# A two-block language-model forward pass on one core: three projection blocks of the next stage are run chunk by chunk while the norm before them arrives, at four boundaries

## Chip, core and metric

The kernel runs on one core of one Trainium2 chip. The metric is device time in microseconds (us) of one launch. TensorE (PE) multiplies matrices, ScalarE (ACT), VectorE (DVE) and GpSimd (POOL) work element by element, and SyncE (SP) issues the loads of the weights.

## What is computed

The reference runs 272 tokens (16 meta tokens and 256 others) of width 1024 through two blocks, all in float32. The first block has a state-space mixer, a latent-attention mixer and two squared-ReLU MLPs. The second block, on 256 tokens, is where the change lies. Cut to what matters:

```python
def second_block(x, mem, ...):
    mem_n = rms_norm_2(mem, mem_norm_gain)              # 256 memory tokens
    for layer in range(2):
        g = norm_gains[layer]
        hn = rms_norm_2(x, g[0])
        y = mlstm_mixer(hn, ...) if layer == 0 else stick_breaking_mixer(hn, ...)
        x = x + rms_norm_2(y, g[1])
        y = memory_cross_attention(rms_norm_2(x, g[2]), mem_n, w_q, w_kv, w_o)
        x = x + rms_norm_2(y, g[3])
        y = swiglu_ffn(rms_norm_2(x, g[4]), w_gate_up, w_down)
        x = x + rms_norm_2(y, g[5])
```

## The kernel before

Activations lie with features on the 128 partitions and tokens along the row, so 1024 features are 8 **chunks** of 128x256. A projection is cut into **blocks** of 128 output features. A block (`pe_block`) is 8 chunks times 3 matmuls of 256 columns: float32 operands are split into a high and a low part, and high x high, high x low and low x high are summed in one PSUM bank. The weights of a block pass through three steps: SP loads 512 KB into one of 4 `RAW` buffers, ACT writes the high part `WH` (`act_split`, signal `hi`), DVE writes the low part `WL` (`dve_split`, signal `lo`). ACT may write slot i mod 4 only when the block four earlier has been used (`use`), and splits up to 3 blocks ahead of the block it is handling; DVE splits 2 ahead. The order of all blocks is one list, `PLAN`.

All synchronisation is by semaphores in an order written by hand for each engine; an engine that waits holds back all that is queued behind it.

A **boundary** is what stands between two stages: a projection `post` (xo0, fd0, sbo, xo1) gives Y in 8 blocks; its squares are summed over features by PE with a matrix of ones (a **product**; `pe_feed` for the early ones, `pe_rest` for the last); ACT takes Ln and Exp of the sum (`act_table`); DVE refines the reciprocal root in three operations (`dve_newton`, signal `rms`). Then for each chunk m, DVE scales Y, DVE (even m) or POOL (odd m) adds it to X, ACT writes the high part of the next norm's input `HNH` and its square, and DVE writes the low part `HNL` (signal `hn`). The next stage's blocks multiply these unscaled chunks, and its own sum of squares (8 more products into bank 7) gives a factor by which DVE multiplies each block when it evicts it. So the next stage's first eviction waits for products, Ln, Exp and the three refining operations again.

While PE would wait at a boundary it is given **fills**: key (k) and value (v) blocks of the memory cross-attention, `xkv0` and `xkv1`, 16 blocks each, which depend on no norm of x. A v block is followed by two transposes (`pe_v_end`). Before the change `xkv1` is dealt out as: k0 and k1 in the last steps of cross-attention 0, k2 to k7 at boundary xo0, v0 to v3 at the end of the stick-breaking mixer, v4 to v7 at boundary sbo. Boundaries fd0 and xo1 have none. The first block of the next stage starts when the five early products of that norm are in.

The stages in order are xq0 and attention core 0, xo0, ffn0 (`gu0` blocks, then `fd0`), `sbqkv` and the stick-breaking core, sbo, xq1 and attention core 1, xo1, ffn1. The first places of the four stages behind the boundaries are blocks gu0 0, sbqkv 0, xq1 0, gu1 0.

## Time and profile before

| | |
|---|---|
| median of 3 runs | 1770.18 us (1765.0 to 1772.51) |
| the profiled execution | 1770.89 us, span 1769.1 us |
| PE busy | 1690.5 us of the span |
| DVE, ACT, POOL busy | 1186.5, 936.5, 332.4 us |
| TensorE clock granted, mean | 0.98 of full |

Time outside the span is 1.8 us. The granted clock is given as a share of 2.4 GHz, so 0.50 in a row is the level of 1.2 GHz. A matmul record lasts longer than the distance to the next one, because matmuls are pipelined; the distance between starts is what a matmul costs. A product of float32 squares is two records.

### The profile page before, as it was taken

The page shows a single profiled execution, that of the slowest core. Times are in us where ns is not written, and L with a number is a line of the kernel's source. Part 1 is how long each engine was busy: PE and PEld are TensorE (multiplying, and loading weights), DVE is VectorE, ACT ScalarE, POOL GpSimd, SP SyncE. Part 2 cuts the span into 40 slices and gives each one's busy share as a digit, 9 for nine tenths or more (in the row PEclk, how much of TensorE's full clock was granted, in tenths as well). Part 3 has the DMA queues.
Part 4 walks back from the last instruction along what each step waited for, and adds up shares of the span by engine and source line. Part 5 has one row for each costly group of instructions (what it writes and reads, how often), then busy time and mean ns, then how long its engine had stood idle before and what let it go on. Part 6 is the DMA issues. An engine that isn't in the chain of part 4 may idle for free.

```text
span 1769.1 us, 32699 instructions
## 1 busy us (share of the span) xinstructions
PE 1690.5 (96%) x13204; PEld 1615.9 (91%) x13204; DVE 1186.5 (67%) x2027; ACT 936.5 (53%) x1659; POOL 332.4 (19%) x304
## 2 busy tenths in 40 slices
PE   6999999999999989999999999999989999989997
PEld 6898889999997889999888999999979998889997
DVE  6999887555577745556577665866666667476665
ACT  5677765544455646544555444544455644454443
POOL 0100011243412112345111100000252110000025
PEclk8999999999999999999999999999999999989999
DMA  5433334555532245555334534455644343335663
GB/s 179 132 120 108 120 108 143 166 171 177 179 93 80 81 140 184 187 187 185 129 118 146 167 120 155 155 170 184 181 147 136 127 156 118 107 118 172 185 184 106
DMA packets 76325, 257.47 MB, mean 146 GB/s; under 512 B 8464, under 2 KB 12560, under 8 KB 75920
## 3 DMA queue, kind: packets, MB, share of 16 engines
q1 hardware_dynamic: 76176, 255.39, 45.1%
q8 instruction: 105, 1.72, 0.4%
q14 instruction: 44, 0.36, 0.1%
HBM read 254.31 MB, written 1.05 MB: 144 GB/s over the span
## 4 chain that ended last, share of the span: by engine, by line
PE 77%; DVE 12%; ACT 6%; issue 4%; POOL 1%; DMA 0%; POOLq 0%; DVEq 0%; SPq 0%; ACTq 0%
PE pb L140 75%; DVE WL L159 2%; DVE TMP L171 2%; DVE SCR L171 2%; ACT SCR L149 1%; ACT L156 1%; DVE SCR L159 1%; PE pb L143 1%; ACT WH L149 1%; DVE HNL L171 1%; POOL SCR L159 1%; ACT TMP L149 1%; ACT ASH L149 1%; DVE ASL L171 0%; ACT Rbuf L149 0%
## 5 line engine op out<-in xcount | busy, mean ns | idle before, releaser
L140 PE MATMUL pb<-HNH,WH 128*128 128x256 f32 (+1 forms) x2120 | 613.9, 290 | 6.1 <-DVE WL L159 1.9
L159 DVE TENSOR_TENSOR WL<-RAW,WH 128x1024 fp32r<-128x1024 f32 (+4 forms) x514 | 604.9, 1177 | 10.4 <-ACT WH L149 10.0
L140 PE MATMUL pb<-HNH,WL 128*128 128x256 f32 (+1 forms) x2120 | 603.1, 284 | 0.0
L140 PE MATMUL pb<-HNL,WH 128*128 128x256 f32 (+1 forms) x2120 | 602.8, 284 | 0.0
L149 ACT ACTIVATE WH<-RAW 128x1024 fp32r<-128x1024 f32 (+4 forms) x514 | 507.2, 989 | 154.7 <-PE pb L140 147.1
L140 PE MATMUL pb<-ASH,WH 128*128 128x256 f32 (+1 forms) x1688 | 493.4, 292 | 11.1 <-DVE WL L159 7.1
L140 PE MATMUL pb<-ASH,WL 128*128 128x256 f32 (+1 forms) x1688 | 483.2, 286 | 0.0
L140 PE MATMUL pb<-ASL,WH 128*128 128x256 f32 (+1 forms) x1688 | 482.9, 286 | 0.0
L140 PEld LDWEIGHTS pb<-HNH,WH 128*128 128x128 f32 x2120 | 402.1, 190 | 14.3 <-issue 6.8
L140 PEld LDWEIGHTS pb<-HNH,WL 128*128 128x128 f32 x2120 | 402.4, 190 | 0.0
L140 PEld LDWEIGHTS pb<-HNL,WH 128*128 128x128 f32 x2120 | 400.6, 189 | 1.0
L140 PEld LDWEIGHTS pb<-ASH,WH 128*128 128x128 f32 x1688 | 324.3, 192 | 19.0 <-issue 7.9
L140 PEld LDWEIGHTS pb<-ASL,WH 128*128 128x128 f32 x1688 | 323.5, 192 | 1.0
L140 PEld LDWEIGHTS pb<-ASH,WL 128*128 128x128 f32 x1688 | 324.1, 192 | 0.0
L140 PE MATMUL pb<-SCR 128*64 128x128 f32 (+12 forms) x880 | 124.5, 321 | 10.7 <-DVE SCR L171 4.2
L140 PEld LDWEIGHTS pb<-SCR 128*64 128x64 f32 (+6 forms) x880 | 91.1, 162 | 34.1 <-issue 11.2
L159 DVE TENSOR_TENSOR ASL<-TMP,ASH 128x256 fp32r<-128x256 f32 (+1 forms) x108 | 46.5, 430 | 109.2 <-ACT ASH L149 109.2
L159 POOL TENSOR_TENSOR SCR<-SCR,TMP 128x256 f32<-128x256 f32 x48 | 59.9, 1248 | 312.9 <-DVE TMP L159 312.9
L159 POOL TENSOR_TENSOR SCR<-SCR 128x512 f32<-128x512 f32 (+2 forms) x36 | 43.5, 1217 | 377.8 <-ACT SCR L149 239.8
L159 POOL TENSOR_TENSOR X<-X,TMP 128x272 f32<-128x272 f32 (+1 forms) x64 | 96.4, 1506 | 87.9 <-DVE TMP L159 87.9
L159 DVE TENSOR_TENSOR TMP<-pb,Rbuf 128x256 f32<-128x256 f32 (+1 forms) x112 | 47.9, 428 | 94.8 <-PE pb L140 94.8
L140 PE MATMUL pb<-SQ,cp 128*128 128x256 f32 (+2 forms) x274 | 83.8, 421 | 25.9 <-ACT SQ L149 22.5
(149 smaller groups left out, 1454.3 us busy)
## 6 DMA issues: line engine op xcount, KB each, us to landing
RAW<-in_w_gu SPq DMA_DIRECT2D x88, 512.0 KB, 3.8
RAW<-in_w_up SPq DMA_DIRECT2D x64, 512.0 KB, 3.5
RAW<-in_w_down SPq DMA_DIRECT2D x64, 512.0 KB, 3.5
RAW<-in_w_ssd SPq DMA_DIRECT2D x48, 512.0 KB, 3.5
RAW<-in_w_xkv SPq DMA_DIRECT2D x32, 512.0 KB, 3.5
RAW<-in_w_mlin SPq DMA_DIRECT2D x24, 512.0 KB, 3.5
RAW<-in_w_fd SPq DMA_DIRECT2D x32, 384.0 KB, 3.0
RAW<-in_w_sbqkv SPq DMA_DIRECT2D x24, 512.0 KB, 4.1
```

The lines of the kernel that those rows point to most:

```text
L140: return self.eng.matmul(o, l, r, start=start, stop=stop, skip_group_check=skip) if self.eng else Nothing()
L143: return self.eng.transpose(o, i, ident) if self.eng else Nothing()
L149: return self.eng.activation(o, i, f, bias=bias, scale=scale)
L156: self.eng.preload_act_table_set(name)
L159: return self.eng.tensor_tensor(o, a, b, op) if self.eng else Nothing()
L171: return self.eng.scalar_tensor_tensor(out=o, in0=a, scalar=s, in1=b, op0=op0, op1=op1)
```

## The change

At the four boundaries xo0, fd0, sbo and xo1, `pe_post_norm` gives way to `pe_wave`. It runs at most one fill, the last products of the post norm, the other fills, and then a **wave**: as each normed chunk c arrives, three matmuls of block 0 and three of block 1 of the next stage on it; from c = 4 on also six matmuls of block 2, on chunks 2c-8 and 2c-7. The waves write PSUM banks 3, 4 and 5, and each waits for that bank's last reader (`wave_free`). The last three products follow the wave. ACT splits one weight block more before the norms (`act_split_to`), DVE one before its refining operations, one behind its first `HNL`, and at the start of the next stage the one for block 3.

The memory blocks `xkv1` are dealt out anew: k0, k1, k2 in the last steps of cross-attention 0; k3, k4 at xo0; k5, k6, k7 at fd0; v0 to v3 as before; v4, v5 at sbo; v6, v7 in the last steps of cross-attention 1. Since the FFN has overwritten the normed memory by then, k5 to k7 read a copy in `ASH`/`ASL` 0 to 7 that `act_mem2` and `dve_mem2` make during the last eight `fd0` blocks: 8 more ACT and 8 more DVE instructions of 128x256. In cross-attention 1 the core no longer waits for v7 at its start; head h waits for value block 2h+1 before its last product.

```diff
     p += xkv[0][0:7] + out("mlo", xkv[0][7:16])
-    p += [("xq0", 0, m) for m in range(8)] + xkv[1][0:2] + out("xo0", xkv[1][2:8])
-    p += ffn(0)
-    p += [("sbqkv", 0, m) for m in range(24)] + xkv[1][8:12] + out("sbo", xkv[1][12:16])
-    p += [("xq1", 0, m) for m in range(8)] + out("xo1", [])
+    p += [("xq0", 0, m) for m in range(8)] + xkv[1][0:3] + out("xo0", xkv[1][3:5])
+    p += ffn(0) + xkv[1][5:8]
+    p += [("sbqkv", 0, m) for m in range(24)] + xkv[1][8:12] + out("sbo", xkv[1][12:14])
+    p += [("xq1", 0, m) for m in range(8)] + xkv[1][14:16] + out("xo1", [])
     p += ffn(1)
...
+WAVES = [(name, m) for name in ("gu0", "sbqkv", "xq1", "gu1") for m in range(3)]
...
-            elif AT["ssd", 0, FIRST] <= i - 3 <= AT["ssd", 0, 47]:
-                q.wait_ge(*ssd_read(i - 4))
+            elif (name, m) in WAVES:
+                for w in wave_free(name, m):
+                    q.wait_ge(*w)
             elif i >= 3:
-                q.wait_ge(*(eva if PLAN[i - 3][0] in ("up0", "up1", "wk") else evd)[i - 3])
+                j = bank_before(i)
+                if AT["ssd", 0, FIRST] <= j <= AT["ssd", 0, 47]:
+                    q.wait_ge(*ssd_read(j - 1))
+                else:
+                    q.wait_ge(*(eva if PLAN[j][0] in ("up0", "up1", "wk") else evd)[j])
...
-                "xo0": [(1, "k", m) for m in range(2, 8)], "sbo": [(1, "v", c) for c in range(4, 8)],
-                "xo1": [], "fd0": [], "fd1": []}
+                "xo0": [(1, "k", 3), (1, "k", 4)], "fd0": [(1, "k", m) for m in range(5, 8)],
+                "sbo": [(1, "v", 4), (1, "v", 5)], "xo1": [], "fd1": []}
+        WAVE = {"xo0": "gu0", "fd0": "sbqkv", "sbo": "xq1", "xo1": "gu1"}
+        def wave_free(name, m):
+            return {"gu0": ([xex[0, 3, 1]], [dm[3]], [xp[0, 3]]),
+                    "sbqkv": ([evd[AT["gu0", 0, 0]]], [evd[AT["gu0", 0, 1]]], [evd[AT["gu0", 0, 2]]]),
+                    "xq1": ([zd[7, 0]], [zd[7, 1]], [xvc[1, 4]]),
+                    "gu1": ([xex[1, 3, 1]], [evd[AT["xq1", 0, 1]]], [xp[1, 3]])}[name][m]
...
+        def pe_wave(q, post):
+            fill, nxt, name = FILL[post], NEXT[post], WAVE[post]
+            for f in fill[:1]:
+                pe_fill(q, *f)
+            pe_rest(q, post, T2)
+            for f in fill[1:]:
+                pe_fill(q, *f)
+            xs = hn_chunks(nxt)
+            ids = [q.block(name, 0, m) for m in range(3)]
+            for c in range(8):
+                for m in range(2):
+                    if c == 0:
+                        pe_bank_free(q, ids[m])
+                        q.wait_ge(*lo[ids[m]])
+                    pe_chunks(q, ids[m], T2, xs, c, c + 1)
+                if c == 4:
+                    pe_bank_free(q, ids[2])
+                    q.wait_ge(*lo[ids[2]])
+                if c > 3:
+                    pe_chunks(q, ids[2], T2, xs, 2 * c - 8, 2 * c - 6)
+                pe_feed(q, nxt, c, T2, rms[post])
+            pe_rest(q, nxt, T2)
...
+        def act_wave(q, post):
+            fill, nxt, name = FILL[post], NEXT[post], WAVE[post]
+            n = POSTS.index(post)
+            for f in fill[:1]:
+                act_fill(q, *f)
+            act_table(q, post, row(RPO, T2), T2, 1024, ynorm[POSTS[n - 1], 7])
+            act_split_to(q, q.i + 3)
+            for m in range(1, 9):
+                act_norm(q, nxt, m - 1, x_added(post, m - 1), use[AT[HNFREE[nxt]]])
+                if m in (2, 4) and m // 2 < len(fill):
+                    act_fill(q, *fill[m // 2])
...
+        def dve_wave(q, post):
+            fill, nxt, gi, name = FILL[post], NEXT[post], GAIN[post], WAVE[post]
+            for f in fill[:1]:
+                dve_fill(q, *f)
+            dve_split_to(q, q.i + 2)
+            r = row(RPO, T2)
+            dve_newton(q, post, r, SUMS[:, 0:T2], 1024, rough[post])
+            q.wait_ge(*rms[post])
+            for m in range(10):
+                if m < 8:
+                    q.wait_ge(*y_ready(post, m))
+                    q.stt(Y[:, m, :], Y[:, m, :], cc("ng", gi * 8 + m, 1), r, ALU.mult, ALU.mult).then_inc(*ynorm(post, m))
+                if m % 2 and m < 8:
+                    d = X[:, m - 1, NMETA:T1]
+                    q.wait_ge(*ynorm[post, m - 1])
+                    q.wait_ge(*x_before(post, m - 1))
+                    q.tt(d, d, Y[:, m - 1, :], ALU.add).then_inc(*xpd(post, m - 1))
+                if m > 1:
+                    dve_norm(q, nxt, m - 2)
+                if m == 2:
+                    dve_split_to(q, q.i + 3)
+                if m in (3, 5) and m // 2 < len(fill):
+                    dve_fill(q, *fill[m // 2])
+                    dve_split_to(q, q.i + 2)
...
+        def act_mem2(q, c):
+            act_part(q, "mem2", c, ASH[:, c, 0:T2], MR[:, c, :], use[AT["fd0_5", 0, 7]], scale=cc("memn", c, 1))
...
         def xa_fill(l, n):
-            return [(1, "k", n - 9)] if l == 0 and n > 8 else []
+            if l == 0:
+                return [(1, "k", n - 8)] if n >= 8 else []
+            return [(1, "v", n - 2)] if n in (8, 9) else []
...
-                    q.wait_ge(*xvc[l, 7])
...
+                q.wait_ge(*xvc[l, 2 * h + 1])
...
-            pe_v_end(q, l, 7)
+            if l == 0:
+                pe_v_end(q, 0, 7)
             for m in range(8):
-                pe_block(q, f"xq{l}", 0, m, T2, xs)
-                if m == 0:
+                if l == 0 or m > 2:
+                    pe_block(q, f"xq{l}", 0, m, T2, xs)
+                if l == 0 and m == 0:
                     pe_rest(q, key, T2)
                 for h, k in xa_cores(m):
                     pe_xa_core(q, l, h, k)
             for n in range(8, 11):
                 for f in xa_fill(l, n):
                     pe_fill(q, *f)
+                if l and n == 10:
+                    pe_v_end(q, 1, 7)
                 for h, k in xa_cores(n):
                     pe_xa_core(q, l, h, k)
-            pe_post(q, f"xo{l}", as_chunks(key, 0, 8, T2, 2), rms[key])
-            pe_post_norm(q, f"xo{l}")
+            pe_post(q, f"xo{l}", as_chunks(key, 0, 8, T2, 2), xvc[1, 7] if l else rms[key])
+            pe_wave(q, f"xo{l}")
...
                         if x == 0:
+                            dve_split_to(q, i + 3)
                             dve_newton(q, key, R, SUMS[:, 0:T2], 1024, rough[key])
                             q.wait_ge(*rms[key])
...
+                            if 2 * (c0 + j) + e > 2:
+                                pe_block(q, f"gu{l}", 0, 2 * (c0 + j) + e, T2, xs)
```

The DVE queue at the start of ffn0 before the change: the refining operations of the norm, the eviction of gate block 0 (`TMP<-pb,Rbuf`), and what follows, with what each row waits for.

```order
L171 SCALAR_TENSOR_TENSOR Rbuf<-TMP,Rbuf 128x256 [waits newton_step]
L171 SCALAR_TENSOR_TENSOR TMP<-pb,Rbuf 128x256 [waits block_done,rms_done]
L171 SCALAR_TENSOR_TENSOR TMP<-TMP 128x256 [waits g_tanh]
L159 TENSOR_TENSOR WL<-RAW,WH 128x1024 [waits w_high]
L159 TENSOR_TENSOR TMP<-TMP,pb 128x256 [waits block_done,g_silu]
L159 TENSOR_TENSOR ASL<-TMP,ASH 128x256 [waits as_high]
L159 TENSOR_TENSOR WL<-RAW,WH 128x1024 [waits w_high]
```

The same place after the change, from the split that stands ahead of the refining operations.

```order
L160 TENSOR_TENSOR WL<-RAW,WH 128x1024 [waits w_high]
L172 SCALAR_TENSOR_TENSOR TMP<-pb,Rbuf 128x256 [waits rms_rough]
L172 SCALAR_TENSOR_TENSOR TMP<-TMP,Rbuf 128x256 [waits newton_step]
L172 SCALAR_TENSOR_TENSOR Rbuf<-TMP,Rbuf 128x256 [waits newton_step]
L172 SCALAR_TENSOR_TENSOR TMP<-pb,Rbuf 128x256 [waits block_done,rms_done]
L172 SCALAR_TENSOR_TENSOR TMP<-TMP 128x256 [waits g_tanh]
L160 TENSOR_TENSOR TMP<-TMP,pb 128x256 [waits block_done,g_silu]
L160 TENSOR_TENSOR ASL<-TMP,ASH 128x256 [waits as_high]
L160 TENSOR_TENSOR WL<-RAW,WH 128x1024 [waits w_high]
```

The split of block 3 has moved from behind the eviction of block 0 to ahead of the refining operations; the last row, in both, is the split of block 4. When the last row before the change runs, PE has blocks 1 to 3 to do behind the norm's products; after the change it has block 3 alone.

The PE queue at the start of cross-attention 1 before the change: the end of block 2 of three (bank 1), the scores of head 0 (`pb3<-SCR`, which need the evictions of the first two blocks), and the next block.

```order
L140 MATMUL pb1<-HNH,WH 128x256
L140 MATMUL pb1<-HNL,WH 128x256
L140 MATMUL pb1<-HNH,WL 128x256
L140 MATMUL pb3<-SCR 128x256 [waits mem_v_copied,evicted_dve]
L140 MATMUL pb3<-SCR 128x256 x3
L140 MATMUL pb2<-HNH,WH 128x256 [waits w_low]
L140 MATMUL pb2<-HNL,WH 128x256
```

The same place after the change: the last matmuls of the wave (bank 5), the products, the scores of head 0, and block 3.

```order
L141 MATMUL pb5<-HNH,WH 128x256
L141 MATMUL pb5<-HNL,WH 128x256
L141 MATMUL pb5<-HNH,WL 128x256
L141 MATMUL pb7<-SQ,cp 128x256 [waits square] x4
L141 MATMUL pb3<-SCR 128x256 [waits evicted_dve]
L141 MATMUL pb3<-SCR 128x256 x3
L141 MATMUL pb0<-HNH,WH 128x256 [waits w_low]
```

The scores now stand directly behind the norm's products, with no block between, and still need two evictions that need the sum of those products.

## Rows read from the trace of the kernel before

**Rows 1.** The page, busy time of each engine.

```profile
PE 1690.5 (96%) x13204; PEld 1615.9 (91%) x13204; DVE 1186.5 (67%) x2027; ACT 936.5 (53%) x1659; POOL 332.4 (19%) x304
```

**Rows 2.** Windows: length, busy us (instructions) of each engine, clock, DMA share, GB/s.

```profile
1580.00:1600.00 20.00, 20.00 (x171) 20.00 (x171) 14.48 (x23) 10.64 (x16) 0.00 (x0) 1.00 0.63 195
```

**Rows 3.** Timeline of PE at boundary xo0: start, length, instruction, how many merged.

```profile
1092.88 0.47 PE L140 MATMUL pb<-ASH,WH 128*128 128x256 f32 x1
...
1096.13 0.47 PE L140 MATMUL pb<-ASH,WH 128*128 128x256 f32 x1
...
1101.99 0.59 PE L140 MATMUL pb<-SQ,cp 128*128 128x256 f32 x2
...
1123.73 0.47 PE L140 MATMUL pb<-HNH,WH 128*128 128x256 f32 x1
```

**Rows 4.** Timeline of PE at boundary fd0; idle before in brackets.

```profile
1309.39 0.59 PE L140 MATMUL pb<-SQ,cp 128*128 128x256 f32 x2
...
1317.67 0.77 PE L140 MATMUL pb<-SQ,cp 128*128 128x256 f32 x1 [4.57 <-ACT SQ L149]
...
1326.83 0.47 PE L140 MATMUL pb<-HNH,WH 128*128 128x256 f32 x1
```

**Rows 5.** Timeline of PE: sbo, tail of attention core 1, xo1.

```profile
1460.08 0.47 PE L140 MATMUL pb<-ASH,WH 128*128 128x256 f32 x1
...
1485.22 0.47 PE L140 MATMUL pb<-HNH,WH 128*128 128x256 f32 x1
...
1515.52 0.66 PE L143 MATMUL pb<-cp,SCR 128*128 128x128 f32 x4
1516.86 3.72 PE L140 MATMUL pb<-SCR 128*128 128x256 f32 x16 [0.69 <-ACT SCR L149]
1523.47 1.12 PE L143 MATMUL pb<-cp,SCR 128*128 128x128 f32 x4 [2.89 <-DVE SCR L165]
...
1528.49 0.78 PE L140 MATMUL pb<-ASH,WH 128*128 128x256 f32 x1
...
1552.70 1.82 PE L140 MATMUL pb<-SQ,cp 128*128 128x256 f32 x6
...
1569.58 0.47 PE L140 MATMUL pb<-HNH,WH 128*128 128x256 f32 x1
```

**Rows 6.** Windows round idle times of PE (columns as in group 2).

```profile
642.00:644.00 2.00, 2.00 (x10) 2.00 (x11) 2.00 (x4) 1.97 (x4) 0.43 (x1) 0.53 0.54 135
644.00:646.00 2.00, 2.00 (x13) 2.00 (x13) 1.72 (x3) 1.76 (x3) 0.89 (x1) 0.61 0.73 193
...
1474.00:1476.00 2.00, 0.20 (x1) 0.23 (x2) 2.00 (x6) 1.16 (x4) 0.84 (x1) 1.00 0.74 242
...
1522.00:1523.00 1.00, 0.00 (x0) 0.00 (x0) 0.37 (x2) 0.56 (x4) 0.00 (x0) 0.89 0.00 0
...
1529.00:1530.00 1.00, 1.00 (x8) 1.00 (x7) 0.28 (x1) 0.91 (x2) 0.00 (x0) 0.70 0.00 0
```

**Rows 7.** Timeline of DVE at boundary fd0: last refining operation, HNL of chunks 0 and 2.

```profile
1315.00 0.42 DVE L171 SCALAR_TENSOR_TENSOR Rbuf<-TMP,Rbuf 128x256 f32<-128x256 f32 x1
...
1317.46 0.47 DVE L171 SCALAR_TENSOR_TENSOR HNL<-X,cp,HNH 128x256 fp32r<-128x256 f32 x1
...
1319.85 0.47 DVE L171 SCALAR_TENSOR_TENSOR HNL<-X,cp,HNH 128x256 fp32r<-128x256 f32 x1
```

**Rows 8.** Timeline of ACT, then of DVE, at the start of ffn0.

```profile
1124.12 0.47 ACT L149 ACTIVATE Rbuf<-pb,cp 128x256 f32<-128x256 f32 x1 [1.28 <-PE pb L140]
...
1127.23 1.05 ACT L149 ACTIVATE WH<-RAW 128x1024 fp32r<-128x1024 f32 x1
1129.29 0.42 ACT L149 ACTIVATE ASH<-TMP 128x256 fp32r<-128x256 f32 x1 [1.00 <-DVE TMP L159]
...
1130.08 1.22 DVE L159 TENSOR_TENSOR WL<-RAW,WH 128x1024 fp32r<-128x1024 f32 x1
```

**Rows 9.** Windows in the last fd0 blocks (columns as in group 2).

```profile
1290.00:1300.00 10.00, 10.00 (x87) 10.00 (x86) 6.22 (x12) 5.20 (x8) 6.83 (x7) 1.00 0.65 187
```

More of the change, by code:

```diff
@@ L307, in bank_of, with bank_before @@
                 return banks[m // 2 % 2]
+            if (name, m) in WAVES:
+                return banks[3 + m]
             return banks[3 if name == "mlao" and m == 3 else i % 3]
+        def bank_before(i):
+            return max(j for j in range(max(0, i - 7), i) if bank_of(j) is bank_of(i))
         def pe_bank_free(q, i):
@@ L1754, in mem_tag, with tbank @@
             return f"mem{l}"
-        def tbank(l):
-            return banks[3] if l == 0 else banks[5]
+        def tbank(l, c):
+            return banks[3] if l == 0 else banks[5 if c < 5 else 7]
         def pe_v_end(q, l, c):
-            b = tbank(l)
+            b = tbank(l, c)
             q.wait_ge(*evd[AT[f"xkv{l}", 0, 8 + c]])
+            if l and c == 5:
+                q.wait_ge(*rms["xa1"])
             if c:
@@ L1773, in dve_v_end @@
             q.copy(VM[:, :, 128 * c:128 * c + 128],
-                   tbank(l)[:, 0:256].rearrange("p (i d) -> p i d", i=2)).then_inc(*xvc(l, c))
+                   tbank(l, c)[:, 0:256].rearrange("p (i d) -> p i d", i=2)).then_inc(*xvc(l, c))
         def pe_fill(q, l, kind, m):
-            pe_block(q, f"xkv{l}", 0, m if kind == "k" else 8 + m, T2, as_chunks(mem_tag(0 if l == 0 or kind == "k" else 1),
-                                                                                 8, 8, T2))
+            if l and kind == "k" and m >= 5:
+                xs = as_chunks("mem2", 0, 8, T2)
+            else:
+                xs = as_chunks(mem_tag(0 if l == 0 or kind == "k" else 1), 8, 8, T2)
+            pe_block(q, f"xkv{l}", 0, m if kind == "k" else 8 + m, T2, xs)
             if kind == "v" and m:
@@ L2336, in dve_cross @@
             R = row(RST, T2)
-            dve_v_end(q, l, 7)
-            dve_norm(q, key, 7)
+            if l == 0:
+                dve_v_end(q, 0, 7)
+                dve_norm(q, key, 7)
             for m in range(8):
@@ L2353, in dve_cross @@
                     dve_fill(q, *f)
+                if l and n == 10:
+                    dve_v_end(q, 1, 7)
                 for h, k in xa_cores(n):
@@ L2373, in gu_free @@
                 return use[AT[f"xo{l}", 0, 7]]
-            return use[AT["xkv1", 0, 7 if l == 0 else 15]]
+            return use[AT["xkv1", 0, 4 if l == 0 else 15]]
         def gu_low(l, x):
@@ L2398, in pe_ffn @@
                             pe_feed(q, post, m, T2, rms[key])
-            pe_post_norm(q, post)
+            if l:
+                pe_post_norm(q, post)
+            else:
+                pe_wave(q, post)
         def act_ffn(q, l):
@@ L2423, in act_ffn @@
                         act_block(q, fd_name(l, q4), q4 % 2, m, T2)
+                        if l == 0 and q4 == 3:
+                            act_mem2(q, m)
                         if q4 == 3:
                             act_square(q, post, m, Y[:, m, :], T2, yadd[l, 3, m])
-            act_post_norm(q, post)
+            if l:
+                act_post_norm(q, post)
+            else:
+                act_wave(q, post)
         def dve_ffn(q, l):
@@ L2456, in dve_ffn @@
                         i, b = dve_block(q, fd_name(l, q4), q4 % 2, m, T2)
+                        if l == 0 and q4 == 3:
+                            dve_mem2(q, m)
                         q.wait_ge(*use[i])
@@ L2465, in dve_ffn @@
                             q.tt(TMP[:, 6 + x % 2, 0:T2], b, R, ALU.mult).then_inc(*evd(i))
-            dve_post_norm(q, post)
+            if l:
+                dve_post_norm(q, post)
+            else:
+                dve_wave(q, post)
         def pool_ffn(q, l):
@@ L2534, in pe_sb @@
             for n in range(24):
-                pe_block(q, "sbqkv", 0, n, T2, xs)
-                if n == 0:
-                    pe_rest(q, "sb", T2)
+                if n > 2:
+                    pe_block(q, "sbqkv", 0, n, T2, xs)
                 for c, k in sb_cores(n):
@@ L2544, in pe_sb @@
             pe_post(q, "sbo", as_chunks("sb", 0, 8, T2), rms["sb"])
-            pe_post_norm(q, "sbo")
+            pe_wave(q, "sbo")
         def act_sb_core(q, c, k):
@@ L2583, in act_sb @@
             act_post(q, "sbo")
-            act_post_norm(q, "sbo")
+            act_wave(q, "sbo")
         def dve_sb_core(q, c, k):
@@ L2634, in dve_sb @@
             dve_post(q, "sbo")
-            dve_post_norm(q, "sbo")
+            dve_wave(q, "sbo")
         def pool_sb(q):
```

25 lines of the change are left out of this document (15 added, 10 removed).

## The prediction

> **What bounds the kernel now.** I read the busy times first: PE is at work 1690.5 of 1769.1 us [rows 1], so the time is the sum of PE's work and of the moments in which PE waits or runs at half clock. The change removes no matmul, so only those moments can change. The page's line on the clock and the gaps in PE's timeline put most of them, from ffn0 on, at the four boundaries and in the tail of attention core 1. I give each a **loss**: time elapsed less the work in it at full clock. Two prices are needed. A dense stretch has 171 matmuls in 20.00 us, 0.117 each [rows 2], so a block of 24 costs 2.81. Between the starts at 1092.88 and 1096.13 lie one block and one product, 3.25 us [rows 3], so a product costs 0.44.
>
> - xo0: 1101.99 to 1123.73, 21.74 us [rows 3], for four fills and one stage block (14.05) and ten products (4.4). Loss 3.3.
> - fd0: 1309.39 to 1326.83, 17.44 us [rows 4], for one block and eleven products (7.65). Loss 9.8; a single wait for a square is 4.57 of it.
> - sbo: 1460.08 to 1485.22, 25.14 us [rows 5], for five blocks (14.05), ten products (4.4) and five pairs of transposes, which I estimate at 0.24 each from the record of four, 0.66 with its drain (1.2). Loss 5.5.
> - Tail of core 1: 1515.52 to 1528.49, 12.97 us [rows 5]. It holds two sets of four transposes (0.5 each), sixteen matmul records (3.5) and eight more, half as much (1.75): 6.25. Loss 6.7, and 0.6 more because the clock comes back only at about 1529.6 [rows 6]: 7.3.
> - xo1: 1552.70 to 1569.58, 16.88 us [rows 5], for 7.65 as in fd0. Loss 9.2.
> - In core 0 the same 0.69 wait as at 1516.86 [rows 5]: 0.7.
>
> Sum 35.8 us, 2.0% of the span. That is the most the change could win there.
>
> **The waves.** At fd0 the last refining operation ends at 1315.42 and the low part of chunk 0 at 1317.93, 2.5 us later; each two chunks more take 2.39 [rows 7]. In the new order DVE has a split of 1.14 (the distance 1.22 less overlap, [rows 8]) behind chunk 0, so I put the low part of chunk 4 at 7.5 us after `rms`; fills add their evictions, 0.34 each. PE can do only 24 of the wave's 72 matmuls on chunks 0 to 3, one fourth at a time. From chunk 4 on each step is 12 matmuls and a product, 1.84: PE becomes the slower one, 7.4 us for four steps, and 1.3 for the last three products. Block 3 of the stage can then start at `rms` + 16.2.
>
> `rms` itself comes 2.3 us after Ln starts (Ln 0.47, Exp and three refining operations 0.42 each, with small gaps, [rows 7, 8]), and Ln starts about 0.4 after PE has issued the last product [rows 3, 8].
>
> - xo0: fill k3 from 1096.13 to 1098.95, products to 1099.8, Ln 1100.1, `rms` 1102.4, block 3 at 1118.6. From 1096.13 that is 22.5 us for five blocks and ten products (18.45). Loss 4.0 against 3.3: six fills hid most of this norm, two do not.
> - fd0: fill k5 covers the last square; products to 1313.5, `rms` 1316.0, two evictions and one more split, block 3 at 1333.7. 24.3 us for six blocks and eleven products (21.7): 2.6. The copy of the memory adds 0.25 (below). Loss 2.9 against 9.8.
> - sbo: `rms` 1466.6, one transposed value copied in between, block 3 at 1483.1. 23.0 us for five blocks, ten products, two pairs of transposes (18.9). Loss 4.1 against 5.5.
> - xo1: no fill, so the wait for chunk 0 stays. `rms` 1556.9, block 3 at 1573.1: 20.4 us for three blocks and eleven products (13.3), 7.1. The clock is down when the wave starts; I add 1.3. Loss 8.4 against 9.2.
> - Tail of core 1: v6 covers the copy, v7 the softmax of 2.89 (a block is 2.81). New waits: 0.65 for value block 5 and some 1.7 for value block 7 behind a split, an eviction, two copies; 0.5 remains. Loss 2.85 against 7.3. Core 0: 0 against 0.7.
>
> Sum 22.3. So far a gain of 35.8 - 22.3 = 13.5 us. Nearest bounds: if DVE's extra split hides, each wave starts its second half 1.15 earlier (4.6 more); if the clock stays down in the xo1 wave, 3.7 less.
>
> **The copy of the memory** is 8 ACT and 8 DVE instructions of about 0.47 in eight blocks of 1.76 us. DVE is at 6.22 of 10.00 and ACT at 5.20 there [rows 9]; 0.40 more per block makes DVE about 85%. It hides, save where a split is 1024 wide. Without that cover it would cost 8 x 0.4 = 3.2.
>
> **What is late next.** This is where the answer turns. The stage behind a wave has its own sum of squares, Ln, Exp and refining. Count from R, the start of that Ln; PE's next block starts at R - 0.39 (1123.73 against 1124.12, [rows 3, 8]). Before, blocks 1 to 3 lay behind R. Now only block 3 is both split and independent of the factor, and it ends at R + 2.4.
>
> - ffn0 and ffn1: ACT's high split of block 4 is queued behind the tanh, at R + 3.1 (1127.23), to R + 4.2. The ASH copy can follow at once, DVE's low part of it, then the low split of block 4. In the rows the split starts 0.79 after ASH and takes 1.22 [rows 8]: R + 6.2. PE waits 3.75 us, twice. Nothing else on PE stands in between; the order rows show it.
> - sbqkv: core step 0 needs the eviction of block 2, which DVE reaches behind two evictions and the low split of block 4: R + 4.6. PE waits 2.15.
> - xq1: the scores stand directly behind the products and need two evictions, R + 3.1. PE waits 3.5.
>
> Sum 13.15 us, as much as the gain. Lower bound: 0 if the order did not bind; upper: 1 us more each if a split is delayed.
>
> **The clock.** PE's wait of 2.89 at 1520.6 drops the granted clock to 0.50 from about 1522.8 to 1529.6 [rows 5, 6], long after PE has work again. A wait that ended at 642 left 3.4 us of half clock [rows 6]. The wait before 1475.80 left none (1.00 in the row at 1474, [rows 6]). So the three waits of 3.5 to 3.75 should each lower it, with 2.2 to 5.5 us of half clock left over behind the wait, costing half of that: 1.1 to 2.8, I take 1.9. Three times 5.7.
>
> The Trainium skill has a rule that speaks against this change, in TensorE: Matmul & The Clock Gate, section HAM oscillation — how this bites in real kernels: do all chunks of one output tile before waiting, so that PE stays warm. The wave does the opposite. By the row at 1474 the wave's gaps alone would cost nothing; by that rule every wave would also run its second half at the lower level (rival 2).
>
> **Sum.** Gain 13.5, waits 13.15, clock 5.7: 5.3 us slower than the profiled execution, whose own time, 1770.89, is its span and 1.8 us around it: 1776.2. The median of the runs is 0.7 below that execution: 1775.5, and since the clock term is the softest I say 1775. Changes of under 0.5% (8.9 us) cannot be told from none.
>
> **Rivals.**
>
> 1. The waits behind the waves do not open, because DVE and ACT reach the splits in time, or PE's wave ends later than I say and the norm's chain catches up less. For it: DVE is idle a third of the time. Against: the queue order. Gain 13.5, time 1757. It decides if block 4 starts within 1 us of block 3's end. Chance 0.17.
> 2. The clock falls in the waves. PE is busy about half the time for five us on chunks 0 to 3, and the second half, 7.4 us, then runs at half clock for 3.4 to 6.8 us, costing 1.7 to 3.4 at each of the three waves that I priced at full clock. With 3.4: 10 us more than the forecast, 1785. For it: half clock after 2.5 us of idleness elsewhere. It decides if the clock row of a wave's second half reads near 0.5. Against: the busy share at 1474 is lower still and the clock holds. Chance 0.21.
> 3. The waits open but the clock holds: 1770, no change. Chance 0.12.
> 4. The forecast, 1770 to 1780: 0.50.
>
> The chances add up to 1. Slower by over 0.5% is rival 2 alone, faster is rival 1 alone; 3 and 4 give 0.62 for within 0.5%. For 8 in 10 the range reaches from 1758 to 1785; the forecast's own range is 1768 to 1780.
>
> **What would show it.** In the profile after: no idle time over 2 us at fd0 and a loss near 3 there; in the tail no wait for the softmax; a wait of PE for WL of some 3.7 us one block behind the waves of ffn0 and ffn1; one of about 3.5 for the evictions (DVE SCR) ahead of the first scores of core 1; a clock of 0.50 behind each. I am wrong if block 4 is ready at R + 2.4, or if the wave runs at 0.50 from its start.

## Result and profile after

The median is 1797.53 us (1795.59 to 1802.42, four runs) against 1767.74 before (four runs; the forecast started from 1770.18, the median of three): ratio 1.017, 95% interval 1.0136 to 1.0204. The forecast was 1775, with a range of its own of 1768 to 1780 and, for 8 in 10, 1758 to 1785. So the kernel is 22.5 us above the forecast time, and the change costs 29.8 us where the forecast's sum had 5.3. The profiled execution took 1802.42 us, its span 1800.6, with a mean granted clock of 0.97.

From the page of the kernel after, the span and the busy times:

```profile
span 1800.6 us, 32706 instructions
...
PE 1703.2 (95%) x13204; PEld 1631.3 (91%) x13204; DVE 1189.5 (66%) x2035; ACT 939.6 (52%) x1667; POOL 334.0 (19%) x304
```

The 13204 matmuls of [rows 1] are still there. PE's busy time grew by 12.7 us without new matmuls, and the span by 31.5; windows at half clock are shown below. The waits of PE, summed by what ended them (total us, times, longest):

```profile
PE pb L141 <- DVE WL L160: 20.9, 10, 3.5
PE pb L141 <- DVE HNL L172: 15.2, 9, 5.0
PE pb L141 <- ACT SQ L150: 9.4, 6, 5.6
...
PE pb L141 <- POOL SQ L160: 5.7, 2, 4.1
...
PE pb L141 <- DVE SCR L160: 3.2, 1, 3.2
```

Before, PE waited 23.7 us for ACT's squares; of the 9.4 left, 5.6 is the first wait of the program, which the change doesn't touch. The waits of 4.6 us at fd0 and xo1 are gone, as the change means them to be, but a square is still awaited for 4.10 us ahead of the fd0 norm, and DVE's weight splits (`WL`) now head the list. PE's timeline shows where; the bracket is the idle time and what ended it. At xo0 and ffn0:

```profile
1109.42 0.36 PE L141 MATMUL pb<-HNH,WH 128*128 128x256 f32 x1 [2.16 <-DVE HNL L172]
...
1112.06 0.58 PE L141 MATMUL pb<-HNH,WH 128*128 128x256 f32 x1 [1.69 <-DVE HNL L172]
...
1132.70 0.55 PE L141 MATMUL pb<-HNH,WH 128*128 128x256 f32 x1 [3.52 <-DVE WL L160]
```

In the last `fd0` blocks and at the boundary behind them, where [rows 9] had PE full:

```profile
1307.93 0.35 PE L141 MATMUL pb<-ASH,WH 128*128 128x256 f32 x1 [1.12 <-DVE WL L160]
...
1311.58 0.35 PE L141 MATMUL pb<-ASH,WH 128*128 128x256 f32 x1 [1.64 <-DVE WL L160]
...
1315.23 0.36 PE L141 MATMUL pb<-ASH,WH 128*128 128x256 f32 x1 [1.17 <-DVE WL L160]
...
1321.34 1.22 PE L141 MATMUL pb<-SQ,cp 128*128 128x256 f32 x2 [4.10 <-POOL SQ L160]
```

Behind the waves of `sbqkv`, `xq1` and `gu1`:

```profile
1356.61 0.48 PE L144 MATMUL pb<-cp,SCR 128*128 128x128 f32 x2 [1.81 <-DVE SCR L160]
...
1512.16 1.99 PE L141 MATMUL pb<-SCR 128*128 128x256 f32 x8 [3.18 <-DVE SCR L160]
...
1607.29 0.55 PE L141 MATMUL pb<-HNH,WH 128*128 128x256 f32 x1 [3.52 <-DVE WL L160]
```

**Accounting by stage.** Two executions do not start alike (the Ln behind `mlo`, the projection that ends the first mixer of the second block and with which the table starts, is at 991.75 to 1002.46 in the profiles of this study), so absolute times cannot be compared. But every norm shows its Ln, `Rbuf<-pb`, on ACT, and the FFN a table load. I take the distance between two such rows before and after, and add or take off 2.815 us (24 matmuls of 0.1173) for each block that now stands on the other side of a row. Two of them after, beside 1124.12 in [rows 8]:

```profile
1126.39 0.48 ACT L150 ACTIVATE Rbuf<-pb,cp 128x256 f32<-128x256 f32 x1 [7.62 <-PE pb L141]
...
1296.40 1.28 ACT L157 ACT_TABLE_LOAD   x1
```

Before, the table load is at 1293.54: 169.42 us behind that Ln. After, the distance is 170.01 with two blocks fewer behind the Ln (5.63), so 6.2 us longer.

| stretch (its last row) | before | after | blocks | longer | forecast |
|---|---|---|---|---|---|
| core 0 and xo0 (Ln of ffn0) | 1001.08 to 1124.12 | 1002.46 to 1126.39 | +1 | 3.7 | 0.0 |
| ffn0 (table load) | to 1293.54 | to 1296.40 | +2 | 6.2 | 5.65 |
| last `fd0` blocks, products (Ln of fd0) | to 1313.13 | to 1330.26 | -1 | 11.5 | -6.9 with the next |
| fd0 wave (Ln of sbqkv) | to 1327.22 | to 1352.00 | -4 | -3.6 | |
| stick-breaking (Ln of sbo) | to 1467.43 | to 1487.02 | +3 | 3.3 | 2.15 |
| sbo (Ln of xq1) | to 1485.61 | to 1509.02 | -1 | 1.0 | -1.4 |
| attention core 1 (Ln of xo1) | to 1554.56 | to 1579.32 | 0 | 1.3 | 0.95 |
| xo1 (Ln of ffn1) | to 1569.97 | to 1600.97 | -2 | 0.6 | -0.8 |
| ffn1 (table load) | to 1739.39 | to 1770.92 | +2 | 6.2 | 5.65 |
| sum | | | | 30.1 | 5.3 |

The sum is that of the unrounded rows. One row of one execution is good to about 1.3 us, where the clock is the same: experiments whose code is alike there differ by that. Where the clock falls in one execution and not in the other, it is less exact: ffn0 differs by 2.6 between two kernels that are alike there (first experiment). Two misses stand out, the last `fd0` blocks with 11.5 us and the three boundaries xo0, sbo, xo1 with 5.3 us instead of a gain of 2.2. The waits behind the waves are nearly as forecast.

### The profile page after: what moved, and what is told of

Its sections match the earlier page's. It is cut to its first block, busy times and chain, and to the rows that moved or that the text cites. A ratio compares the mean times of both kernels' runs of the same rounds, so it can differ in the third digit from the quotient of the medians.

```text
span 1800.6 us, 32706 instructions
## 1 busy us (share of the span) xinstructions
PE 1703.2 (95%) x13204; PEld 1631.3 (91%) x13204; DVE 1189.5 (66%) x2035; ACT 939.6 (52%) x1667; POOL 334.0 (19%) x304
## 4 chain that ended last, share of the span: by engine, by line
PE 72%; DVE 13%; ACT 6%; issue 6%; POOL 2%; DMA 0%; POOLq 0%; DVEq 0%; ACTq 0%; SPq 0%
PE pb L141 71%; DVE WL L160 3%; DVE TMP L172 3%; POOL SCR L160 2%; DVE SCR L172 2%; DVE SCR L160 1%; ACT SCR L150 1%; ACT WH L150 1%; ACT L157 1%; PE pb L144 1%; ACT Rbuf L150 1%; DVE HNL L172 1%; ACT ASH L150 1%; ACT TMP L150 1%; DVE ASL L172 0%
## 5 line engine op out<-in xcount | busy, mean ns | idle before, releaser
L141 PE MATMUL pb<-HNH,WH 128*128 128x256 f32 (+1 forms) x2120 | 622.9, 294 | 28.4 <-DVE HNL L172 15.2
L160 DVE TENSOR_TENSOR WL<-RAW,WH 128x1024 fp32r<-128x1024 f32 (+4 forms) x514 | 603.8, 1175 | 11.5 <-ACT WH L150 11.3
L141 PEld LDWEIGHTS pb<-HNH,WH 128*128 128x128 f32 x2120 | 407.2, 192 | 39.7 <-issue 24.3
L141 PEld LDWEIGHTS pb<-HNL,WH 128*128 128x128 f32 x2120 | 406.3, 192 | 1.4
L141 PEld LDWEIGHTS pb<-HNH,WL 128*128 128x128 f32 x2120 | 407.4, 192 | 0.0
L141 PEld LDWEIGHTS pb<-ASH,WH 128*128 128x128 f32 x1688 | 326.4, 193 | 24.8 <-issue 7.9
L150 ACT ACTIVATE ASH<-TMP 128x256 fp32r<-128x256 f32 (+1 forms) x108 | 45.5, 422 | 116.4 <-DVE TMP L160 66.7
```

The costliest lines, as they stand in the source:

```text
L141: return self.eng.matmul(o, l, r, start=start, stop=stop, skip_group_check=skip) if self.eng else Nothing()
L150: return self.eng.activation(o, i, f, bias=bias, scale=scale)
L160: return self.eng.tensor_tensor(o, a, b, op) if self.eng else Nothing()
```

## What happened in the last fd0 blocks

The instructions that come round once per block, ACT first, then DVE and POOL:

```profile
1308.41 0.42 ACT L150 ACTIVATE SQ<-SCR 128x256 f32<-128x256 f32 x1 [2.20 <-POOL SCR L160]
1308.73 0.72 ACT L150 ACTIVATE WH<-RAW 128x640 fp32r<-128x640 f32 x1
1309.36 0.49 ACT L150 ACTIVATE ASH<-SCR,cp 128x256 fp32r<-128x256 f32 x1
```

```profile
1309.88 0.48 DVE L172 SCALAR_TENSOR_TENSOR ASL<-SCR,cp,ASH 128x256 fp32r<-128x256 f32 x1 [2.10 <-ACT ASH L150]
1310.29 0.42 DVE L160 TENSOR_TENSOR TMP<-pb,Rbuf 128x256 f32<-128x256 f32 x1
```

```profile
1310.78 1.24 POOL L160 TENSOR_TENSOR SCR<-SCR,TMP 128x256 f32<-128x256 f32 x1 [2.41 <-DVE TMP L160]
```

The next square is at 1312.05. Read in a circle: the square waits for POOL's sum, the sum for DVE's eviction `TMP`; the eviction needs nothing more, but it stands in DVE's queue behind the low part of the copy (`ASL`), which waits for ACT's high part (`ASH`); and this stands in ACT's queue behind the weight split and the square of the block before. The new instructions have tied two chains that did not touch into one **ring**. A turn takes 3.65 us (squares at 1301.10, 1304.76, 1308.41, 1312.05, 1315.70), and it is the sum of its members, from start to start: square 0.32, ACT's weight split 0.63, high part 0.52, low part 0.41, eviction 0.49, POOL's addition 1.27, together 3.64. DVE's weight splits, for which PE waits, hang in the same queue as the eviction. PE's work for one turn is 1.76. Both engines are idle 2.1 to 2.2 us in each turn, as the brackets show, and the kernel still goes at half its pace.

## Experiments

The ratio stands against runs of the kernel before on the same chip, taken beside those of the experiment, with its 95% interval. Where I say how many us less than the change, two medians taken at different times are compared, and with four runs each interval is about 5 us to either side; so I give the distance between rows of the profiled executions beside it, from the `mlo` row to that of the FFN's last table load, corrected as in the table.

**The low part one block later.** DVE makes the low part of chunk m - 1 in block m, so the eviction no longer stands behind a high part that is not yet begun.

```diff
-                        if l == 0 and q4 == 3:
-                            dve_mem2(q, m)
+                        if l == 0 and q4 == 3 and m:
+                            dve_mem2(q, m - 1)
...
+                dve_mem2(q, 7)
                 dve_wave(q, post)
```

> The changed kernel with one thing moved: in the last eight fd0 blocks DVE writes the low part of memory chunk m one block later, behind block m+1's start. Theory A (a ring in the order of the queues: DVE's eviction of block m waits for its low part of the copy, that for ACT's high part, that stands in ACT's queue behind the square of block m-1, that waits for POOL's addition, and that for the eviction of block m-1; 3.65 us a round where PE needs 1.77): the ring opens, the blocks come at 1.8 us again, some 15 us less than the changed kernel's 1797.5, about 1783. Theory B (the load of the 16 added instructions, or too little cover, costs): they are all still there, so 1795 or more.

Measured 1784.34 us, ratio 1.0088 (1.0061 to 1.0115): 13.2 us less than the change as made, with the same instructions. Between the rows it is 15.0 less, and 10.6 of that lie here: the stretch of 11.5 us is down to 0.9. Most of the rest has nothing to do with the move. At ffn0 and in `sbqkv`, where the two kernels are alike and PE waits as long (3.51 and 1.81 us), this execution kept its clock at 1.00 and is 2.6 and 1.5 us shorter ("The clock behind them" below). The squares come in pairs again, 1.43 and 3.24 apart; [rows 9]'s window holds one more copy per block and PE is full:

```profile
1299.42 0.42 ACT L150 ACTIVATE SQ<-SCR 128x256 f32<-128x256 f32 x1 [1.78 <-POOL SCR L160]
1300.85 0.42 ACT L150 ACTIVATE SQ<-SCR 128x256 f32<-128x256 f32 x1
```

```profile
1290.00:1300.00 10.00, 10.00 (x86) 10.00 (x85) 8.26 (x13) 6.10 (x12) 6.42 (x6) 1.00 0.62 187
```

DVE is at 83%, the load I had forecast (85%), and it does no harm. The order did.

**No copy.** The instructions of the copy are left out, and k5 to k7 read other chunks, so the values of these three blocks are not the reference's.

```diff
             if l and kind == "k" and m >= 5:
-                xs = as_chunks("mem2", 0, 8, T2)
+                xs = (as_chunks(("gu", 0, 2), 0, 5, T2) * 2)[:8]
...
-                        if l == 0 and q4 == 3:
-                            act_mem2(q, m)
...
-                        if l == 0 and q4 == 3:
-                            dve_mem2(q, m)
```

> The changed kernel without the copy of the normed memory; key blocks 5 to 7 of memory 1 multiply five chunks of the gated product instead, so their values are not the reference's. Theory A: 15 us less than the changed kernel, about 1782.5, the same as with the low part moved, since only the ring cost. Theory B: less than with the low part moved by what the 16 instructions cost as load. Theory C (it is the weight loads or the fills at fd0, not the copy): no gain, 1797.

Measured 1781.52 us, ratio 1.0079 (1.0049 to 1.0108). The stretch is now 2.2 us shorter than before, since k5 covers the last square. So as made the copy costs 13.7 us there, one block later still 3.1. The median is within 1 us of the first theory's 1782.5; the 3.1 leave the second, the load of the sixteen instructions, a small share.

**The ring by itself.** The kernel before, with the copy alone, in the changed kernel's order; nothing reads it.

```diff
                         act_block(q, fd_name(l, q4), q4 % 2, m, T2)
+                        if l == 0 and q4 == 3:
+                            act_mem2(q, m)
...
                         i, b = dve_block(q, fd_name(l, q4), q4 % 2, m, T2)
+                        if l == 0 and q4 == 3:
+                            dve_mem2(q, m)
```

> The kernel before with nothing but the copy of the memory added, in the order of the changed kernel; its result isn't used by anything. Theory A (ring): the eight blocks take 3.65 us each instead of 1.77, 13 to 15 us more than before, 1780 to 1783. Theory B (it needed the fills or the waves to hurt): under 3 us more, 1771 at most.

Measured 1782.8 us, ratio 1.0095 (1.0077 to 1.0113): sixteen instructions of half a microsecond cost 16.5 us by the medians (13.6 to 20 by the interval) in a kernel that is otherwise the one before. Between the rows, the stretch of the last `fd0` blocks is 13.8 longer, the same as in the changed kernel, and all other stretches are within 0.9. So the ring needs neither waves nor fills. The squares are 3.65 apart here too (1296.83, 1300.48, 1304.13, 1307.78), and PE waits as in the changed kernel:

```profile
1300.01 0.36 PE L140 MATMUL pb<-ASH,WH 128*128 128x256 f32 x1 [1.13 <-DVE WL L159]
...
1303.66 0.36 PE L140 MATMUL pb<-ASH,WH 128*128 128x256 f32 x1 [1.63 <-DVE WL L159]
...
1313.41 1.11 PE L140 MATMUL pb<-SQ,cp 128*128 128x256 f32 x2 [4.09 <-POOL SQ L159]
```

**Block 2 behind the wave.** The third block of each wave is multiplied whole behind the products of the next norm, as cover for that norm's Ln, Exp and refining.

```diff
-                if c == 4:
-                    pe_bank_free(q, ids[2])
-                    q.wait_ge(*lo[ids[2]])
-                if c > 3:
-                    pe_chunks(q, ids[2], T2, xs, 2 * c - 8, 2 * c - 6)
                 pe_feed(q, nxt, c, T2, rms[post])
             pe_rest(q, nxt, T2)
+            pe_bank_free(q, ids[2])
+            q.wait_ge(*lo[ids[2]])
+            pe_chunks(q, ids[2], T2, xs, 0, 8)
```

> The changed kernel with block 2 of each wave multiplied whole behind the three last products, in place of its pairs of chunks in the wave. Theory A (the waits of 3.52, 1.81, 3.18 and 3.52 us behind the waves come from there being one block of cover, and each lowers the clock): the waits shrink to about 1, 0, 0.5 and 1, the clock stays at 1.00 behind them, and the wave itself ends no later. 9.5 us of waits and 6 to 8 of clock less: about 1781. Theory B (the norm's chain is late anyway, the wait only moves ahead into the wave's second half, which now has half the work): less than 5 us, 1793 or more.

Measured 1777.47 us, ratio 1.0055 (1.0034 to 1.0076): 20.1 us less than the change as made, and 18.8 between the rows: 5.3 at ffn0, 3.6 in `sbqkv`, 4.4 in core 1, 5.3 at ffn1. The wait at ffn0 falls from 3.52 to 0.68, as does that of ffn1; the clock is 1.00 round it where it was 0.50. The wait for the scores of core 1 falls from 3.18 to 0.34, and the one in `sbqkv` is gone.

```profile
1123.70 0.36 PE L141 MATMUL pb<-HNH,WH 128*128 128x256 f32 x1 [0.68 <-DVE WL L160]
```

```profile
1123.00:1125.00 2.00, 1.32 (x12) 1.33 (x12) 1.52 (x4) 1.07 (x2) 0.00 (x0) 1.00 0.19 33
```

The forecast's wait of 3.75 rests on one block of cover. With block 2 behind the products as well, the wait and the half clock behind it are both gone, as the first theory had it.

**A split later in the wave.** DVE's weight split, 1.14 us that stand ahead of the low parts of chunks 1 to 7, moves behind the low part of chunk 4, except at fd0.

```diff
-                if m == 2:
-                    dve_split_to(q, q.i + 3)
+                if m == (2 if post == "fd0" else 6):
+                    dve_split_to(q, q.i + 2 if post in ("xo0", "sbo") else q.i + 3)
                 if m in (3, 5) and m // 2 < len(fill):
                     dve_fill(q, *fill[m // 2])
-                    dve_split_to(q, q.i + 2)
+                    if post == "fd0":
+                        dve_split_to(q, q.i + 2)
```

> The changed kernel with DVE's split behind the first low part moved behind the fifth at xo0, sbo and xo1 (at fd0 it stays). Theory A (the split holds back chunk 1, PE waits twice within 3.5 us at the start of each wave, and that lowers the clock to 0.50 in the waves of xo0 and sbo): the second wait shrinks from 1.7 to about 0.5, the clock holds there, 2.5 us less per wave and 1 at xo1: about 1791. Theory B (the first wait of 2 us lowers the clock by itself): 0 to 2 us, 1796.

Measured 1790.11 us (1782.64 to 1790.71), ratio 1.0118 (1.0089 to 1.0146): 7.4 us less than the change, but the two intervals overlap, and its four runs lie 8 us apart. What carries the gain is the profiled execution, the fastest of the four, which shows the three boundaries 2.0, 1.8 and 2.1 us shorter. The total is near the first theory's 1791, its mechanism only in part: the second wait at xo0 is 0.46 instead of 1.69, but the clock still falls in the wave. It is back about three and a half microseconds later:

```profile
1100.00:1102.00 2.00, 1.54 (x8) 1.24 (x7) 2.00 (x5) 1.49 (x4) 0.53 (x1) 0.51 0.00 0
1102.00:1104.00 2.00, 2.00 (x12) 1.90 (x12) 2.00 (x5) 1.30 (x4) 0.85 (x1) 0.64 0.00 0
1104.00:1106.00 2.00, 2.00 (x17) 1.94 (x17) 2.00 (x4) 0.23 (x1) 0.06 (x1) 1.00 0.00 0
```

In the change as made it stays down from about 1111.5 to 1117.7:

```profile
1110.00:1112.00 2.00, 0.37 (x4) 0.17 (x2) 2.00 (x5) 0.82 (x3) 0.84 (x1) 0.78 0.30 66
1112.00:1114.00 2.00, 1.94 (x9) 1.94 (x10) 2.00 (x7) 0.80 (x3) 0.40 (x1) 0.50 0.50 197
1114.00:1116.00 2.00, 2.00 (x10) 1.90 (x10) 2.00 (x5) 1.42 (x4) 0.46 (x1) 0.50 0.00 0
1116.00:1118.00 2.00, 2.00 (x10) 1.82 (x9) 1.98 (x4) 1.70 (x5) 0.84 (x1) 0.51 0.03 8
```

DVE is busy in 2.00 of 2.00 us of nearly every one of these windows: the first half of a wave goes at DVE's pace, and each split put into it is time of PE.

**The moves together.** First those of the first and third experiment (the low part later, block 2 behind), then with the later split as well; the edits are the ones shown.

> The changed kernel with the low part of the memory copy one block later and block 2 of each wave behind the products. If the ring and the missing cover are two causes, their gains add: 13.2 and 20.1 us less than 1797.5, about 1764, level with before. If they shared a cause (the clock that one pulls down for the other), the sum falls short: 1770 or more.

> As the kernel with both moves, and also DVE's split at xo0, sbo and xo1 behind the fifth low part. Theory A (the clock falls in the waves for the two waits at their start): the 7.4 us that this move gave alone are left in full, about 1757, 0.5% faster than before. Theory B (with block 2 behind the products DVE paces the wave and the norm's chain follows it, so the move gains more at the end of the wave): 1754. Theory C (part of its gain lay in the second half of the wave, which is gone now): 1761.

Two moves: 1766.4 us, ratio 0.9985 (0.9971 to 0.9999). Three: 1762.48, ratio 0.9974 (0.996 to 0.9987), a quarter of a per cent faster than before and 35 us faster than the change. From 1797.5 the single gains of 13.2 and 20.1 would give 1764.3; 1766.4 was measured. Between the rows two moves bring 29.2, which is 10.6 for the low part's stretch and 18.8 for block 2. So they are two separate losses that add up. The third move brings 3.9 by the medians, whose intervals overlap, and 3.3 between the rows, about half of what it gave alone; of its three theories the last, at 1761, comes nearest. Before, a square was awaited for 4.57 us at fd0 [rows 4], and as long at xo1:

```profile
1559.10 3.97 PE L140 MATMUL pb<-SQ,cp 128*128 128x256 f32 x8 [4.58 <-ACT SQ L149]
```

With three moves these two waits are replaced by waits for chunks, the longest at xo1, where no fill stands (of the squares, 5.3 is again the first wait of the program):

```profile
PE pb L141 <- DVE HNL L172: 15.9, 14, 5.0
PE pb L141 <- DVE WL L160: 10.7, 8, 2.6
PE pb L141 <- ACT SQ L150: 7.7, 5, 5.3
```

**The tail of core 1 alone.** The kernel before, with v6 and v7 moved into the last steps of core 1 and the core's wait for v7 split by head.

```diff
-    p += [("sbqkv", 0, m) for m in range(24)] + xkv[1][8:12] + out("sbo", xkv[1][12:16])
-    p += [("xq1", 0, m) for m in range(8)] + out("xo1", [])
+    p += [("sbqkv", 0, m) for m in range(24)] + xkv[1][8:12] + out("sbo", xkv[1][12:14])
+    p += [("xq1", 0, m) for m in range(8)] + xkv[1][14:16] + out("xo1", [])
...
-                    q.wait_ge(*xvc[l, 7])
...
+                q.wait_ge(*xvc[l, 2 * h + 1])
```

> The kernel before with one part of the change alone: value blocks 6 and 7 of memory 1 in the last steps of attention core 1 instead of at sbo, no wave, nothing else moved. By the prediction's steps: tail 4.5 us better; sbo has two fills fewer and loses what they hid, up to 2 x 2.8. If the two cancel, 1765 to 1768, as before. If the tail's gain holds alone: 1762.

Measured 1765.61 us, ratio 0.9987 (0.9974 to 1.0001), not to be told from no change, and in the range expected if the two parts cancel. Core 1 is 1.9 us shorter, boundary sbo 1.9 longer for its two missing fills.

**All blocks dealt out anew, no waves.** The same, with k2 to k7 moved too, and the copy with its low part later.

```diff
-    p += [("xq0", 0, m) for m in range(8)] + xkv[1][0:2] + out("xo0", xkv[1][2:8])
-    p += ffn(0)
+    p += [("xq0", 0, m) for m in range(8)] + xkv[1][0:3] + out("xo0", xkv[1][3:5])
+    p += ffn(0) + xkv[1][5:8]
```

> The kernel before with the whole new dealing of the memory blocks, the low part of the copy one block later, and no wave. It says what the waves are worth: if the waves bring what their first matmuls hide, this kernel is 5 to 10 us slower than the one with both moves (1770 to 1774). If the fills do the work and the waves bring nothing, it is level with it (1764).

Measured 1768.97 us, ratio 1.001 (0.9995 to 1.0024). Dealing out by itself wins nothing: xo0 is 5.9 us longer without four of its fills (the wait of 4.58 for a square opens there as well), and fd0, sbo, core 1 and xo1 together give 2.2 of it back in the profiled execution. Against the two moves together, which differ from this kernel by the waves, the waves are worth 2.6 us (2.8 between the rows), where 5 to 10 or nothing had been expected; the third move makes it some 4 more.

**The copy earlier.** The kernel with three moves, two chunks of the copy per block in the first four of the eight `fd0` blocks, so that the last four, in which ACT and DVE have the squares and splits of the boundary, carry none.

```diff
-                        if l == 0 and q4 == 3:
-                            act_mem2(q, m)
+                        if l == 0 and q4 == 3 and m < 4:
+                            act_mem2(q, 2 * m)
+                            act_mem2(q, 2 * m + 1)
...
-                        if l == 0 and q4 == 3:
-                            dve_mem2(q, m)
+                        if l == 0 and q4 == 3 and 0 < m < 5:
+                            dve_mem2(q, 2 * m - 2)
+                            dve_mem2(q, 2 * m - 1)
```

> As the kernel with the three moves, with the copy of the memory made two chunks per block in the first half of the last eight fd0 blocks, low parts one block later. In the kernels with the low part one block later PE still waits 1.1 us for a paired square and 1.4 us for the last low part in fill k5. If both come from ACT's copy of chunks 4 to 7 standing among the squares, they vanish: 2 to 2.5 us less, about 1760. If not, or if two copies in a block delay a weight split instead: 1762.5 or more.

Measured 1763.49 us, ratio 0.9986 (0.9974 to 0.9998); the interval overlaps that of the three moves (0.996 to 0.9987). PE's waits there are 0.58 and 1.73 instead of 1.11 and 1.41, about the same sum. The 3.1 us that the copy costs one block later are not won by moving it again; what they consist of beyond these two waits is open.

## Why the prediction was wrong

Step by step, in us. The bounds below come from the table by stage and its counterparts in the experiments.

- **The copy of the memory: the step that failed.** "It hides, save where a split is 1024 wide" priced it at 0.25, without cover at 3.2. It cost 13.7 at that place in the changed kernel and 13.8 there by itself (16.5 by the medians), over four times the upper bound. Both figures were loads, so much work on engines so busy; the load came out right (83%), the conclusion did not. The kernel's order puts the low part ahead of the eviction on DVE and the high part behind the square before on ACT, and I did not ask whose signal each one stands behind. The same question, asked for block 4 behind the waves, gave right numbers.
- **The waits behind the waves: right.** Forecast 3.75 (ffn0), 2.15 (`sbqkv`), 3.5 (`xq1`) and 3.75 (ffn1), sum 13.15; measured 3.52, 1.81, 3.18 and 3.52, sum 12.0. Rival 1 falls.
- **The clock behind them: right in sum, and that in part by luck.** The three stretches ffn0, `sbqkv` and ffn1 are longer by 2.7, 1.5 and 2.6 beyond the wait, 6.8 against 5.7. But the half clock is not where I put it throughout: it follows the waits of ffn0, ffn1 and `sbqkv` (1.81 us only, 0.50 at 1358), and not the wait of 3.18 for the scores, behind which the row reads 1.00.

```profile
1358.00:1360.00 2.00, 2.00 (x12) 1.74 (x9) 0.35 (x2) 1.24 (x3) 0.00 (x0) 0.50 0.74 260
...
1514.00:1516.00 2.00, 2.00 (x18) 2.00 (x17) 0.86 (x2) 0.88 (x4) 0.00 (x0) 1.00 0.76 250
```

  Other executions have it otherwise at the same waits. With the low part later, the clock stayed at 1.00 behind 3.51 at ffn0 and behind 1.81 in `sbqkv`:

```profile
1129.10 0.36 PE L141 MATMUL pb<-HNH,WH 128*128 128x256 f32 x1 [3.51 <-DVE WL L160]
```

```profile
1130.00:1132.00 2.00, 2.00 (x20) 2.00 (x19) 1.66 (x3) 0.99 (x2) 0.00 (x0) 1.00 0.72 254
```

  With the split later, it fell behind the same 3.18 for the scores:

```profile
1495.71 3.55 PE L141 MATMUL pb<-SCR 128*128 128x256 f32 x8 [3.18 <-DVE SCR L160]
```

```profile
1496.00:1498.00 2.00, 2.00 (x6) 1.58 (x6) 1.12 (x2) 0.00 (x0) 0.00 (x0) 0.50 0.07 8
```

  So the length of a wait of 1.8 to 3.5 us didn't settle whether the half clock follows; up to 2.7 us hang on it at each place, and a forecast can give them only as a mean.

- **The waves at xo0, sbo, xo1: too cheap.** Core 0 and these boundaries were to win 2.2 and lost 5.3. "By the row at 1474 the wave's gaps alone would cost nothing" is the weak sentence: that row had one long gap (2.29, then 0.59 and 0.98), a wave has two (2.16 and 1.69 at xo0, 1.94 and 1.70 at sbo, 4.99 and 1.02 at xo1) with between 0.9 and 1.7 us of work between them, and the clock is 0.50 for 5 to 6 us of work behind the second; at xo1 it had fallen within the first, as forecast. That is rival 2 (chance 0.21, 1.7 to 3.4 us a wave) only in part: it had the half clock on the wave's second half, but it lay on chunks 1 to 3 and the start of chunk 4, and the rest of the second half ran at 1.00. Two terms of the wave were too small. DVE's low part of chunk 4 ends 8.8, 9.1 and 8.4 us behind `rms` at xo0, sbo and xo1, where I had 7.5: 3.8 in sum. And PE, slowed on chunks 1 to 3, takes chunk 4 up late, at xo0 1.2 us behind its low part:

```profile
1115.06 0.47 DVE L172 SCALAR_TENSOR_TENSOR HNL<-X,cp,HNH 128x256 fp32r<-128x256 f32 x1
```

```profile
1116.74 0.78 PE L141 MATMUL pb<-HNH,WH 128*128 128x256 f32 x1
```

  At sbo it is 1.2 and at xo1 1.4 us late, at fd0, with the clock at 1.00, 0.05; and from there to the last products PE takes 7.7, 7.5 and 7.6 us where fd0 takes 7.1. That is 5.3 in sum, of which I had 1.3 at xo1. The two together are 7.8, for a miss of 6.8 at the three boundaries; in core 0 the 0.7 to be won did not come, because a wait of 1.06 took the place of the one of 0.69. The later split took 5.9 off the three boundaries: the low part of chunk 4 is 1.1 earlier at each, 3.4 together, and the remaining 2.5 are left for the clock that is back sooner. The Trainium skill's rule in TensorE: Matmul & The Clock Gate, section HAM oscillation — how this bites in real kernels, which I had set against the row at 1474, speaks against such a loop order, and the trace agrees in part: in three of four waves the clock was 0.50, on chunks 1 to 3, and back at 1.00 within chunk 4. In the wave of fd0, whose gaps are 0.62 and 0.87 at most, it held at 1.00.
- **fd0: right but for the copy.** Without the copy both fd0 stretches together are 5.9 shorter, forecast 6.9 + 0.25. So k5 covers the last square, as I had it.
- **The tail of core 1:** forecast 4.45 shorter, measured 1.9, in the changed kernel (1.3 less the wait of 3.18) and in the run of the tail alone. Waits of 0.67, 1.23 and 0.56 remain, and in the changed kernel the clock falls right behind the last:

```profile
1549.58 0.41 PE L144 MATMUL pb<-cp,TMP 128*128 128x128 f32 x2 [1.23 <-DVE SCR L175]
```

```profile
1552.00:1554.00 2.00, 2.00 (x8) 1.73 (x7) 0.00 (x0) 0.51 (x2) 0.00 (x0) 0.50 0.00 0
```

I had put 0.5 of wait there and no half clock. With block 2 behind the wave, the same three waits left the clock at 1.00, and core 1 without its wait for the scores is 3.4 shorter; so of the 2.5 that the tail misses, about 1.5 is the half clock. The wait for the softmax (2.89, [rows 5]) is gone, as forecast.

The sum closes: waits behind the waves and their clock 18.8 (forecast 18.85), the ring's stretch 11.5, all the rest -0.2; for these last two together the forecast had -13.5. The 30.1 are the profiled executions without their offset at the start; the medians differ by 29.8. Of the miss of 24.8 against the sum of 5.3, the copy is 13.5, the three boundaries with core 0 are 7.5, the tail is 2.5 and fd0 without the copy 1.2.

## To carry to other kernels

Where engines run hand-ordered queues, don't price a new instruction by the engine's load: write down what it waits for, what stands behind it, and follow both until the path ends or meets itself; a circle through the queues sets the pace at the sum of its members, and the engines in it still show idle time. A block run early to fill one norm is gone as cover for the next: count the independent work behind each wait after the change, and leave one block there. In a wave, each weight split in the queue of the engine that feeds PE's chunks is time of PE, and short waits there can bring the half clock with them (1.2 to 1.4 us late at chunk 4 in three waves here); put the splits behind the chunks that PE waits for.
